# The opening of a fused decoder layer on one core: larger pieces of x, two weight units by halves, the high parts first

## The reference

```
h = rmsnorm(x, pre_norm_g)
proj = h @ w_in                      # 2048 x 18776, its columns split over three mixers and gates
y_a = diff_attention(...) * silu(z)  # 8 heads
y_b = mlstm(...) * silu(z)           # 4 heads, chunkwise
y_c = dsa_attention(...) * silu(z)   # indexer top-64, latent attention
mixed = sum(sigmoid(gate_i) * (y_i @ w_branch[i]))
x = x + rmsnorm(mixed @ w_out, post_norm_g)
```

## Time and profile before

| | us |
|---|---|
| median of 3 runs | 1094.7 |
| lowest, highest | 1094.49, 1095.58 |
| profiled execution, its own time | 1095.71 |
| profiled execution, span of the instructions | 1094.0 |
| TensorE busy | 1083.3 (99%) |
| VectorE busy | 794.4 (73%) |
| ScalarE busy | 536.4 (49%) |

### The profile page before, as it was taken

The page is one execution under the profiler, slowest core; times in us unless marked ns, Lnnn a source line. Parts: engine busy times, 40 slices in busy tenths (PEclk is TensorE's granted clock), DMA queues, the critical chain, the costliest instruction groups (busy, mean ns, idle before and its releaser), DMA issues.

```text
span 1094.0 us, 14575 instructions
## 1 busy us (share of the span) xinstructions
PE 1083.3 (99%) x5057; PEld 898.5 (82%) x5057; DVE 794.4 (73%) x1385; ACT 536.4 (49%) x744; POOL 27.2 (2%) x45
## 2 busy tenths in 40 slices
PE   8999999999999999999999999999999999999997
PEld 7898888888887888889887778888888888888886
DVE  5555566688878887778957777878788777777445
ACT  5664444555555555545455444454444444436442
POOL 0000000000000001111100000000000000000000
PEclk9999999999999999999999999999999999999999
DMA  8776666565666646657665555654655567765552
GB/s 276 199 226 193 193 193 193 174 188 174 192 174 178 182 145 192 201 173 217 198 182 178 173 164 183 210 174 133 197 172 170 145 219 256 235 195 183 194 194 109
DMA packets 114120, 205.82 MB, mean 188 GB/s; under 512 B 11228, under 2 KB 18456, under 8 KB 113688
## 3 DMA queue, kind: packets, MB, share of 16 engines
q1 hardware_dynamic: 114032, 205.21, 61.4%
q10 hardware_dynamic: 40, 0.01, 0.0%
HBM read 203.10 MB, written 2.10 MB: 188 GB/s over the span
## 4 chain that ended last, share of the span: by engine, by line
PE 95%; DVE 4%; ACT 1%; issue 0%; DMA 0%; DVEq 0%; ACTq 0%
PE stream L1476 29%; PE stream L1478 29%; PE stream L1477 29%; PE stream L1597 2%; DVE wlo L875 1%; PE mixer L1722 1%; PE stream L1598 1%; DVE mixed L866 1%; DVE area L1114 0%; ACT whi L562 0%; PE mixer L1738 0%; PE mixer L1689 0%; PE mixer L1511 0%; PE mixer L1688 0%; PE mixer L1575 0%
## 5 line engine op out<-in xcount | busy, mean ns | idle before, releaser
L562 ACT ACTIVATE whi<-raw 128x1024 fp32r<-128x1024 f32 (+1 forms) x376 | 395.4, 1054 | 519.4 <-PE stream L1478 484.6
L875 DVE TENSOR_TENSOR wlo<-raw,whi 128x1024 fp32r<-128x1024 f32 (+1 forms) x376 | 456.6, 1218 | 260.8 <-ACT whi L562 257.6
L1476 PE MATMUL stream<-whi,xboth 128*128 128x512 f32 (+1 forms) x1248 | 491.1, 394 | 0.4 <-DVE wlo L875 0.3
L1478 PE MATMUL stream<-whi,xboth 128*128 128x512 f32 (+1 forms) x1248 | 484.3, 388 | 0.0
L1477 PE MATMUL stream<-wlo,xboth 128*128 128x512 f32 (+1 forms) x1248 | 483.8, 388 | 0.0
L1476 PEld LDWEIGHTS stream<-whi,xboth 128*128 128x128 f32 x1248 | 234.6, 188 | 51.7 <-issue 5.3
L1478 PEld LDWEIGHTS stream<-whi,xboth 128*128 128x128 f32 x1248 | 234.5, 188 | 48.8
L1477 PEld LDWEIGHTS stream<-wlo,xboth 128*128 128x128 f32 x1248 | 234.8, 188 | 45.9
L1476 PE MATMUL stream<-whi,yhi 128*128 128x512 f32 x192 | 76.6, 399 | 0.2 <-DVE ylo L1318 0.2
L1478 PE MATMUL stream<-whi,ylo 128*128 128x512 f32 x192 | 74.9, 390 | 0.0
L1477 PE MATMUL stream<-wlo,yhi 128*128 128x512 f32 x192 | 74.8, 390 | 0.0
(11 more groups left out here) (241 smaller groups left out, 560.8 us busy)
## 6 DMA issues: line engine op xcount, KB each, us to landing
raw<-in_w_in SPq DMA_DIRECT2D x286, 512.0 KB, 3.7
raw<-in_w_branch SPq DMA_DIRECT2D x48, 512.0 KB, 4.6
raw<-in_w_out SPq DMA_DIRECT2D x32, 512.0 KB, 3.7
raw<-in_w_in SPq DMA_DIRECT2D x12, 256.0 KB, 3.3
mixed<-in_x SPq DMA_DIRECT2D x8, 256.0 KB, 6.8
area<-in_x SPq DMA_DIRECT2D x2, 1024.0 KB, 7.7
out<-area SPq DMA_DIRECT2D x8, 256.0 KB, 2.3
raw<-in_dsa_w_uv SPq DMA_DIRECT2D x4, 256.0 KB, 2.9
```

The source lines that it names most:

```text
L562: nc.scalar.activation(whi[:, slot, :, 0:width], raw[:, slot, :, 0:width], ACT.Copy).then_inc(whi_ready, 1)
L875: nc.vector.tensor_tensor(wlo[:, slot, :, 0:width], raw[:, slot, :, 0:width], whi[:, slot, :, 0:width].bitcast(F32), ALU.subtract).then_in ...
L1476: nc.tensor.matmul(to, left_hi[:, kt, tokens], high, start=first, stop=False)
L1478: last = nc.tensor.matmul(to, left_lo[:, kt, tokens], high, start=False, stop=final)
```

## The change

x comes in five pieces, two of 256 columns and three of 512 (rows of 2 KB). Unit 2 and unit 3 are issued together behind the third piece. ACT and DVE take the first weight half before the first tile of x, and then alternate tile of x and weight half. TensorE multiplies units 0 and 1 by `multiply_early`, half by half, high by high first, each pair of matmuls behind its own wait; `turn_x(1)` stands behind the first half, `turn_x(2)` behind the third, `turn_x(3)` behind the fourth. For b from 2 to 7 ACT rounds unit b behind `x_high` of the same b, and DVE splits it behind `x_low`. The idle transposes are 9, 2 and 4.

```diff
-X_LOADS = 8
-X_COLS = D_MODEL // X_LOADS
+X_COLS = D_MODEL // 8
+X_PIECES = [(0, 1), (1, 2), (2, 4), (4, 6), (6, 8)]
+EARLY = 2
...
-            return M[3] if k == 1 else x_banks[k // 2]
+            return {1: M[3], 3: M[0]}.get(k, x_banks[k // 2])
...
-            for u in range(2, 4):
-                load_x(u)
+            load_x(2)
+            load_first(2)
+            load_first(3)
+            for n in range(3, 5):
+                load_x(n)
+                load_first(n + 1)
+            for u in range(6, FULL_UNITS):
                 load_first(u)
-            for n in range(4, 6):
-                load_x(n)
-            for u in range(4, FULL_UNITS):
-                load_first(u)
-                if u < 6:
-                    load_x(u + 2)
...
-            for j in range(2):
+            round_half(0, 0)
+            for j in range(UNIT_KT):
                 act.wait_ge(x_turned, j + 1)
                 x_high(j)
-                round_half(0, j)
-            for b in range(1, 8):
-                if b >= 4:
-                    round_unit(PA0, 0, b - AHEAD)
-                act.wait_ge(x_turned, b + 2)
+            round_half(0, 1)
+            for j in range(UNIT_KT):
+                act.wait_ge(x_turned, UNIT_KT + j + 1)
+                x_high(UNIT_KT + j)
+                round_half(1, j)
+            for b in range(EARLY, FULL_UNITS):
+                act.wait_ge(x_turned, b + 3)
                 for k in range(2 * b, 2 * b + 2):
                     x_high(k)
-                if b == 1:
-                    for j in range(2):
-                        round_half(1, j)
-                elif b < 4:
-                    round_unit(PA0, 0, b - AHEAD)
+                round_unit(PA0, 0, b - AHEAD)
```

DVE's list changes in the same way. On TensorE:

```diff
-                halves = part is PA0 and k < 2
-                if not halves:
-                    pe.wait_ge(wlo_ready, part.unit(i, k) + 1)
+                pe.wait_ge(wlo_ready, part.unit(i, k) + 1)
...
+            def multiply_early(u, j):
+                kt = UNIT_KT * u + j
+                high, low = whi[:, u, j, :], wlo[:, u, j, :]
+                def times(left, right):
+                    for t in range(TILES):
+                        last = nc.tensor.matmul(stream[0][t][:, :], left[:, kt, t * P:(t + 1) * P], right,
+                                                start=kt == 0 and left is xhi and right is high, stop=False)
+                    return last
+                pe.wait_ge(xhi_ready, kt + 1)
+                pe.wait_ge(whi_ready if j else half_whi, u + 1)
+                times(xhi, high)
+                if kt == 0:
+                    pe.wait_ge(half_wlo, 1)
+                    times(xhi, low)
+                    pe.wait_ge(xlo_ready, 1)
+                    last = times(xlo, high)
+                else:
+                    pe.wait_ge(xlo_ready, kt + 1)
+                    times(xlo, high)
+                    pe.wait_ge(wlo_ready if j else half_wlo, u + 1)
+                    last = times(xhi, low)
+                if j == UNIT_KT - 1:
+                    last.then_inc(units_done, 1)
...
-            keep_busy(4)
+            keep_busy(9)
...
-            keep_busy(5)
+            keep_busy(2)
...
-            keep_busy(6)
+            keep_busy(4)
+            multiply_early(0, 0)
             turn_x(1)
-            for u in range(FULL_UNITS):
-                pe.wait_ge(xlo_ready, UNIT_KT * u + (1 if u == 0 else 2))
+            multiply_early(0, 1)
+            multiply_early(1, 0)
+            turn_x(2)
+            multiply_early(1, 1)
+            turn_x(3)
+            for u in range(EARLY, FULL_UNITS):
+                pe.wait_ge(xlo_ready, UNIT_KT * u + 2)
```

More of the change, by code:

```diff
@@ L304, in build @@
         iq_banks = [stream[(iq_group0 + j // 2) % 2][j % 2] for j in range(4)]
-        x_landed = [sem(f"x_landed{n}") for n in range(X_LOADS)]
+        x_landed = [sem(f"x_landed{n}") for n in range(len(X_PIECES))]
         rows_landed, g_landed = sem("rows_landed"), sem("g_landed")
@@ L397, in load_x @@
             def load_x(n):
-                part_of_x = slice(n * X_COLS, (n + 1) * X_COLS)
+                part_of_x = slice(X_PIECES[n][0] * X_COLS, X_PIECES[n][1] * X_COLS)
                 sp.dma_start(x_sb[:, :, part_of_x], x_d[:, :, part_of_x]).then_inc(x_landed[n], 16)
@@ L903, in split_half @@
                                         ALU.subtract).then_inc(wlo_ready if j else half_wlo, 1)
-            for j in range(2):
+            split_half(0, 0)
+            for j in range(UNIT_KT):
                 x_low(j)
[L907 to L910, removed]
+            split_half(0, 1)
+            for j in range(UNIT_KT):
+                x_low(UNIT_KT + j)
+                split_half(1, j)
+            for b in range(EARLY, FULL_UNITS):
                 dve.wait_ge(xhi_ready, 2 * b + 2)
@@ L913, in _ @@
                     x_low(k)
[L914 to L918, removed]
+                split_unit(PA0, 0, b - AHEAD)
             for u in range(FULL_UNITS - AHEAD, FULL_UNITS):
@@ L1462, in multiply @@
                 slot = (part.unit0 + k) % RING
-                halves = part is PA0 and k < 2
-                if not halves:
-                    pe.wait_ge(wlo_ready, part.unit(i, k) + 1)
+                pe.wait_ge(wlo_ready, part.unit(i, k) + 1)
                 for j in range(UNIT_KT):
-                    if halves:
-                        pe.wait_ge(xlo_ready, UNIT_KT * k + j + 1)
-                        pe.wait_ge(wlo_ready if j else half_wlo, k + 1)
                     kt = UNIT_KT * u + j
@@ L1495, in keep_busy @@
                     nc.tensor.transpose(stream[0][1][:, 0:P], ident[:, :], ident[:, :])
-            keep_busy(4)
+            keep_busy(9)
             pe.wait_ge(g_landed, 16)
             nc.tensor.transpose(M[0][:, 0:KT], rows_g[:, :], ident[0:KT, 0:KT]).then_inc(cols_turned, 1)
-            keep_busy(5)
+            keep_busy(2)
             def turn_x(b):
-                pe.wait_ge(x_landed[b], 16)
+                pe.wait_ge(x_landed[b if b < 2 else b // 2 + 1], 16)
                 if b == 4:
-                    pe.wait_ge(cols_ready, 1)
+                    pe.wait_ge(xlo_ready, 4)
                 if b >= 5:
@@ L1508, in turn_x @@
                 for j in range(2):
+                    if b == 1 and j == 1:
+                        pe.wait_ge(cols_ready, 1)
                     for t in range(TILES):
@@ L1512, in turn_x @@
                                                    x_sb[:, t, kt * P:(kt + 1) * P], ident[:, :])
-                    if b == 0 or j == 1:
+                    if b < 2 or j == 1:
                         last.then_inc(x_turned, 1)
             turn_x(0)
-            keep_busy(6)
+            keep_busy(4)
+            multiply_early(0, 0)
             turn_x(1)
-            for u in range(FULL_UNITS):
-                pe.wait_ge(xlo_ready, UNIT_KT * u + (1 if u == 0 else 2))
+            multiply_early(0, 1)
[5 more added lines that the diff above has]
+                pe.wait_ge(xlo_ready, UNIT_KT * u + 2)
                 multiply(PA0, 0, u, u, FULL_UNITS, 0, xhi, xlo)
```

## The result

| | before | changed |
|---|---|---|
| median, 20 runs each | 1094.89 us | 1096.63 us |
| lowest to highest | 1094.49 to 1096.02 | 1096.15 to 1098.54 |
| profiled execution, own time / span | 1095.71 / 1094.0 | 1096.33 / 1094.3 |

Ratio 1.0015, 95% interval 1.0009 to 1.0022: 1.7 us slower, within the 0.2% that was called no change. The forecast was 1096.4.

The account below looks back on a forecast made before the run. TensorE, busy 99% of the span, was taken as the bound. Against the profiled 1095.71 us, unit 2's shift (-0.5 to +1.05) plus late rounding (+1.0) gave +0.5 to +2.05; with the clock rising at 7.2, +0.7: 1096.4 us, range 1095.0 to 1097.8.

Parts of the forecast that it names:

- What bounds it: Whole kernel: TensorE, busy 99% of the span; time unit 8 starts late or early passes whole to the end.
- The reading of the earlier trace: Opening of the kernel before: TensorE's only wait after its first work is 0.3 us for wlo of unit 2.
- Part 1: First matmuls, unit 0: first matmul at 6.7 instead of 8.02 us, with xlo's making hidden.
- Part 2: Turn 2 behind 18 matmuls, not 12: 1.6 us idle before unit 2; 0.5 earlier if clock risen, 1.05 later if not.
- Part 3: Late rounding of units 4 to 7: 0.27 lost before units 4 and 6, 0.44 before 7; 1.0 us in sum.
- Part 4: Transfers of x and weights in the new order: cost 0, pieces and units landing before they are wanted.
- The clock: TensorE's rise to full pace in the opening: taken at about 7.2 us, each us of half pace behind 6.7 costing 0.46.
- The sum: Whole time against the profiled execution before: +0.5 to +2.05 us by the clock's rise, +0.7 taken, 1096.4 us.
- sum for a risen clock: Whole time if the clock has risen by 6.7: -0.5 + 1.0 = +0.5 us, 1096.2.
- The idle transposes: Nine instead of four ahead of pre_norm_g in the kernel before: median 0.2 to 0.5 us lower.
- the early start carries through: Rival, unit 2: starts at 13.6 or 15.1, 2.0 or 0.5 us ahead; 1093.7 to 1095.2 us; chance 0.08.
- The late clock: Rival, opening: clock rises late despite the idle transposes; 1097.0 to 1097.9 us; chance 0.25.

Follow-up runs that it names:

- e12: e8 run again unaltered (changed kernel, turn 2 early, early rounding, eight pieces of x): 1094.41 us, ratio 0.9993 to the kernel before.
- e3: Changed kernel with turn 2 moved one half unit ahead, behind 12 matmuls instead of 18: 1095.86 us, ratio 1.0006 to the kernel before.
- e4: Changed kernel with turn 2 one half unit ahead and units 4 to 7 rounded ahead of their turn: 1095.02 us, ratio 1.0000 to the kernel before.
- e7: Changed kernel with x in eight pieces and the old order of transfers: 1097.10 us, ratio 1.0018 to the kernel before.
- e6: Changed kernel without any idle transposes (0, 0 and 0 instead of 9, 2 and 4): 1099.09 us, ratio 1.0036 to the kernel before.
- e9: Kernel before with nine idle transposes ahead of pre_norm_g instead of four: 1094.68 us, ratio 0.9993 to the kernel before.
- e10: Changed kernel with four idle transposes ahead of pre_norm_g instead of nine: 1097.79 us, ratio 1.0024 to the kernel before.
- e5: Changed kernel run again unaltered: 1096.63 us, ratio 1.0015 to the kernel before.
- e1: Kernel before with only the late rounding (units 4 to 7 rounded and split behind x_high and x_low of the same number): 1096.52 us, ratio 1.0010.
- e2: Changed kernel with late rounding undone (units 4 to 7 rounded ahead of the wait for their turn): 1095.89 us, ratio 1.0007 to the kernel before.
- e8: Changed kernel with turn 2 early, early rounding, and x in eight pieces in the old order of transfers: 1094.67 us, ratio 0.9992 to the kernel before.

## Why the prediction was right

- **What bounds it.** Right for the span, nearly: TensorE's last matmul is 0.33 later than before where the opening left it 0.27 late. In other traces up to 0.4 us were lost between the opening and the end (e12's last one is 1.82 early, out of 2.04). But the whole differs by 0.37 more than the span, which the prediction put at nothing without a word. It is there in every kernel with the new order, with five pieces of x and with eight, with and without idle transposes, late rounding or the late turn 2; so none of these makes it alone, and its cause stays open.
- **The reading of the earlier trace rows.** Wrong: its 0.3 us is a wait at 405 us. That unit 2 stood for about 0.3 is true all the same, by the distances; the two numbers agree by luck.
- **Part 1.** Right but for 0.4: first matmul at 6.29 against 6.7; 0.3 of it is the first weight half, which landed 3.9 us after its issue instead of 4.2. No wait for `wlo` shows among the first matmuls.
- **Part 2.** Right: turn 2 at 11.03 (11.3 worked out for the risen clock), unit 2 at 14.86 (15.1), 3.83 between them (3.82), idle 1.41 by the record and 1.65 by the distance (1.6). e3 showed that the place of turn 2 makes it.
- **Part 3.** Right: stands before units 4, 6 and 7 and none before 3 and 5; 0.93 in the traces, 0.8 to 1.2 by the medians, 1.0 worked out.
- **Part 4.** Right for the changed kernel: the first 512 KB piece landed at 9.6 (9.9 worked out) and unit 2 at 11.2 (11.4), while turn 2 came at 11.03 and ACT took unit 2 at 12.39. In e4, with turn 2 at 9.78, unit 2's transfer set ACT's start. e7's median leaves 0.5 us open.
- **The clock.** Half of it was an assumption: that the runs differ by the moment of the rise and that the five transposes moved ahead bring it forward. e6 shows that idle transposes bring it forward, without an overlap; e9 and e10 show it for the five by their medians. I took a rise at 7.2; in the profile after it came at about 5.5, and in e5's, an execution of 1096.63 like the median, at about 6.6.
- **The sum, and where luck helped.** The sum for a risen clock had +0.5 over the profiled execution of before. The profile after is that case: +0.3 in the span, since turn 2 came 0.3 sooner than worked out, and +0.32 outside it. So its +0.62 agrees with +0.5 because two misses, of 0.2 and 0.3, cancel. It is the same with the forecast: the median is 0.92 over that execution where I had 0.7, but only 0.55 of it lies in the span. The waits were right one by one; that the total came within 0.2 us is partly luck.
- **The idle transposes.** Their effect alone was sized too small before e9: 0.2 to 0.5 expected, 0.70 measured.
- **The rivals.** That the early start carries through is refuted by the 1.41 us wait. The late clock is what e6 shows; the changed kernel's three longest runs (1098.14, 1098.50, 1098.54) have the time that it would give, but no trace shows it for them.

Put together, over the kernel before: late rounding +1.1 (e1, e2), turn 2 +0.9 to 1.2 (e3), idle transposes ahead -0.7 to -1.0 (e9, e10). That is +1.0 to +1.6, and +1.4 to +2.0 with the 0.37 outside the span, against the measured 1.5 to 1.7. What is left for the high parts first and the first matmul 1.7 us sooner is small and not measured alone: e4, with both losses undone, has the span of e9 (1092.9), which is one digit changed in the kernel before, and e12, with smaller pieces besides, is 0.6 under it (1092.3). Of that 0.6, 0.37 is lost again outside the span.

## What to carry to other kernels

An earlier first matmul is worth only what the next chain lets through: before work is put in front of a step that starts a chain on other engines, count what is left on the bound engine to cover the chain, and move the starting step ahead of the new work. When a ring of units keeps up by a few tenths of a us, follow the recurrence over two units rather than one, because a stand in every second unit hardly shows as a wait. If the runs of a kernel scatter by about 1 us, look at the pace of the first matmuls before the scatter is called noise: five idle transposes in an idle stretch took 0.7 us off the median (e9). And when two programs are compared, set the difference of the whole time beside the difference of the spans: what the spans don't have is in no timeline.

## What the runs showed of the hardware

- Back-to-back transposes of a 128x128 float32 identity bring TensorE from 1.2 to 2.4 GHz: in the changed kernel the pace doubled at about 5.5, inside them, with no matmul of 512 columns before; without them it doubled at about 11.6 (e6). These are paces: the granted clock in the profile reads 1.00 on either side of the rise, in every stretch between 1 and 13 us (in the kernel before, also between 8 and 10, where a matmul of 512 columns takes 0.43 us).
- The moment of the rise differs between executions of one kernel. In e8's profiled execution, which took 1096.35 us, two matmuls at 7.93 still last 1.05 us (timeline of e8 below); in e12, the same kernel, the same two last 0.63 and the execution took 1094.25. (The first matmul was also 0.5 later in e8, 6.91 against 6.40.)

```profile
7.93 1.05 PE L1490 MATMUL stream<-wlo,xboth 128*128 128x512 f32 x2
8.78 1.05 PE L1490 MATMUL stream<-whi,xboth 128*128 128x512 f32 x2
```

- The time of an execution outside the span of its instructions goes with the program: 1.67 to 1.80 us in every run of the kernel before, e1 and e9, 2.03 to 2.17 in every run of the changed kernel and its variants.
